# A hybrid decoder step: group norm moved into the next head pair's scan, and the last job cut into two token halves

## Chip, cores and metric

The kernel runs on one core of a Trainium2 chip. The metric is the device time of one execution in microseconds.

## The reference, cut to what matters

One inference step of one decoder layer, in float32, over 544 tokens (512 of a prompt, and 8 samples of 4 tokens). The width is 1024. Three branches run on the same normalised input: sparse attention (A), RWKV-7 time mixing (B) and cross attention into 256 memory tokens (C). Their outputs pass sigmoid gates and an output matrix, then a squared-ReLU MLP of width 4096 and a last RMS norm. The change touches branch B and the last norm:

```
def step(S, inp):                               # per head, 8 heads of 64
    sa = einsum('bhvk,bhk->bhv', S, -kk_t)
    S = S*w_t + sa (x) (kk_t*a_t) + v_t (x) k_t
    return S, einsum('bhvk,bhk->bhv', S, r_t)   # y
yn  = (y - mean(y)) * rsqrt(var(y) + GN_EPS) * ln_g + ln_b     # per head: "group norm"
out = (yn + sum(r*k*r_k)*v) * g                 # the sum term is the "bonus"
...
y_p = h_p + square(relu(rmsnorm(h_p, norm_mlp_g) @ w_mlp_up)) @ w_mlp_down
y_prompt = rmsnorm(y_p, norm_final_g)
```

## The kernel before

Activations lie with features on the 128 partitions and tokens along the free dimension (TOK = 544, HALF = 272, C = 64 tokens to a chunk, NCH = 8 chunks). Each engine has its own hand-written program, and they meet only through counting semaphores (`s["name"]`), so an engine that waits holds up all that is written behind the wait on that engine.

**Jobs.** All large matmuls are jobs of `JOBS`, each of 128 output features: `pb` (the RWKV projections), `gate` (24), `branch`, `out`, `up` and `down` (32, alternating in groups of 8). From `pb 6` on they are split: a weight slab lands by DMA, ScalarE makes its high part (`weights_hi`, L563), and GpSimd (`early_lo`, L577, up to the first `branch` job) or VectorE (`weights_lo`, L571, behind that) the low part, and every k tile takes three matmuls (L980 to L982; behind the scans L1539, L1540, L1543).

**Fills.** The `pb` and `gate` jobs of this region are not run in one piece. `fill_plan` cuts them into steps (one k tile of one half of the tokens, three matmuls of 272 columns for a split job) and deals them out over named places ("tags") in TensorE's program by a table of budgets; `fill(tag)` issues them. ScalarE moves a finished half out of PSUM in `evacs(tag)` (L1652 for the gates) at the matching place of its own program, and issues the `weights_hi` of a later job there; `split_tags` picks those places, and GpSimd calls `early_lo` for the same tags, between its other work, in order.

**The scan.** Branch B loops over four pairs of heads, j = 0 to 3. For each pair TensorE runs: *prep* (fills "prep" 0, 1, 3, 2, with the block sum of `rk` between them), the *pair stage* (matmuls of 64x64 that build and invert the chunk matrices, L1334 to L1415), the *chunks* (per chunk a chain: z matmuls L1424/L1428, ScalarE copies zs L1883, u matmuls L1437, ScalarE copies us L1888, state matmuls L1442, VectorE updates the state L2308, next chunk; with three fills each), the *decode stage* of the samples ("dec", L1466 to L1510, five fills) and *gn*, the group norm. `early(j + 1, ...)` makes the first inputs of the next pair in the chunks. `wide` (L1283) is a 128x128 float32 matmul over all tokens, and is used for block sums and small projections; its results lie in the PSUM pairs 0, 4 or 6.

**Group norm** (tag "gn"): TensorE `wide` of y (mean), VectorE subtracts (`yc`, L2346), ScalarE squares (L1914), TensorE `wide` (var), ScalarE square root (L1917), VectorE reciprocal (L2348), product (L2349), gain and shift (L2350), adds the bonus (L2351) and multiplies by g (L2353, `oB_out`). Behind that `oB_out` GpSimd begins `diff(r_, j + 1)` (L828 to L832) and behind its `diff` VectorE runs `mix` (L2176, L2179), the cumulative scan of the decays (L2252), the chunk offsets (L2256 to L2261, `lx`), ScalarE four exponentials (L1850 to L1853, `exps`), VectorE `rk` (L2264) and the factors (L2265 to L2269), TensorE the `rk` sum, VectorE the bonus (L2271), and only then the pair stage of the next pair.

**The end.** The last job (`down 31`) adds into its tile of `xT3` in one piece (L2417). ScalarE squares that tile, VectorE adds the squares of the tiles up (`add_square`, L1983), TensorE sums over partitions with a matrix of ones (L931), ScalarE takes the square root of all 128x544 (L1618), VectorE the reciprocal (L1965) and eight products (L1974), and SyncE stores each tile (L749).

## Time and profile before

| | us |
|---|---|
| median of three runs | 1272.91 |
| lowest, highest | 1270.98, 1279.83 |
| the profiled execution, its own time | 1272.74 |
| its span in the profile | 1271.1 |

The profile is of one execution; its own time is the span and 1.6 us around it. Stretches are given in microseconds from the start of the span. "PE" is TensorE's matmuls, "PEld" its weight loads, DVE is VectorE, ACT ScalarE, POOL GpSimd, SP SyncE. PEclk is the share of full clock (2.4 GHz) that TensorE was granted; 0.5 is 1.2 GHz. Idle time in brackets stands ahead of the instruction, with the one that released it.

### The profile page before, as it was taken

Reading aid. Unit: us, or ns where it says so; the run is one execution under the profiler, and the core shown is the slowest. Engines: PE = TensorE matmul, PEld = TensorE weight load, DVE = VectorE, ACT = ScalarE, POOL = GpSimd, SP = SyncE. Lnnn points to the kernel's source line nnn. Section 1 sums busy time; section 2 is a strip of 40 time slices with the busy share of each in tenths; the row PEclk is TensorE's granted clock in tenths of the full one; section 3 lists DMA queues with packets and bytes.
Section 4 is the critical chain, followed back from the end, with each engine's and each line's share of the span. In section 5 each row is a group of like instructions: output and inputs, shape, how many; then the busy total and the mean of one; then the engine's idle time right before and its main releaser. Section 6 shows DMA issues by size and latency. Waiting matters only on the chain.

```text
span 1271.1 us, 26790 instructions
## 1 busy us (share of the span) xinstructions
PE 1209.3 (95%) x11356; PEld 1077.9 (85%) x11359; DVE 661.1 (52%) x1190; ACT 385.7 (30%) x743; POOL 181.3 (14%) x218
## 2 busy tenths in 40 slices
PE   7999999898999899889989999999999999999994
PEld 5777665585887888887888899999999999999994
DVE  4898778440634534544362466656554254354334
ACT  2211333343532334333333342233232122122121
POOL 0414000111442242231142200000000000000000
PEclk9999999999999999989999999999999999999997
DMA  8234533233101111201211156522222222222101
GB/s 309 80 121 151 166 114 133 80 137 117 35 19 61 60 53 62 102 11 60 96 68 36 45 189 221 199 96 71 92 75 100 80 87 101 70 97 100 67 34 71
DMA packets 39178, 122.82 MB, mean 97 GB/s; under 512 B 5282, under 2 KB 16546, under 8 KB 30482
## 3 DMA queue, kind: packets, MB, share of 16 engines
q1 hardware_dynamic: 37106, 116.01, 26.2%
q0 software_dynamic: 1952, 5.09, 1.2%
q8 instruction: 90, 1.47, 0.5%
q14 instruction: 30, 0.25, 0.1%
HBM read 109.18 MB, written 11.90 MB: 95 GB/s over the span
## 4 chain that ended last, share of the span: by engine, by line
PE 86%; DVE 7%; issue 2%; ACT 2%; POOL 1%; DMA 1%; SPq 0%; DVEq 0%; ACTq 0%; POOLq 0%
PE ps L1540 13%; PE ps L1543 13%; PE ps L1539 13%; PE ps L989 7%; PE ps L980 5%; PE ps L947 5%; PE ps L981 3%; PE ps L982 3%; PE ps L1283 2%; PE ps L1107 2%; PE ps L1334 1%; PE ps L987 1%; PE ps L984 1%; PE ps L1371 1%; PE ps L1347 1%
## 5 line engine op out<-in xcount | busy, mean ns | idle before, releaser
L563 ACT ACTIVATE wh<-land 128x1024 fp32r<-128x1024 f32 (+1 forms) x125 | 122.1, 977 | 360.3 <-PE ps L1543 360.3
L571 DVE TENSOR_TENSOR wl<-land,wh 128x1024 fp32r<-128x1024 f32 (+1 forms) x94 | 103.3, 1099 | 149.7 <-ACT wh L563 149.0
L980 PE MATMUL ps<-xghi,wh 128*128 128x272 f32 x464 | 151.6, 327 | 9.8 <-ACT R L1652 8.5
L1539 PE MATMUL ps<-xhi,wh 128*128 128x272 f32 x512 | 138.3, 288 | 0.0
L1540 PE MATMUL ps<-hl,wh 128*128 128x272 f32 x512 | 138.2, 289 | 0.0
L1540 PE MATMUL ps<-xlo,wh 128*128 128x272 f32 x512 | 138.2, 289 | 0.0
L1539 PE MATMUL ps<-hh,wh 128*128 128x272 f32 x512 | 138.1, 288 | 0.0
L981 PE MATMUL ps<-xlo,wh 128*128 128x272 f32 x464 | 135.1, 291 | 0.0
L982 PE MATMUL ps<-xghi,wl 128*128 128x272 f32 x464 | 134.9, 291 | 0.0
L980 PEld LDWEIGHTS ps<-xghi,wh 128*128 128x128 f32 x464 | 88.9, 192 | 23.6 <-issue 14.3
L1543 PE MATMUL ps<-xhi,wl 128*128 128x272 f32 x512 | 106.1, 288 | 0.0
L1543 PE MATMUL ps<-hh,wl 128*128 128x272 f32 x512 | 106.1, 288 | 0.0
L577 POOL TENSOR_TENSOR wl<-land,wh 128x1024 fp32r<-128x1024 f32 (+1 forms) x31 | 73.1, 2359 | 226.6 <-ACT wh L563 226.6
L989 PE MATMUL ps<-xn,ring 128*128 128x272 f32 x384 | 98.2, 398 | 0.9 <-ACT aq L1769 0.9
L1540 PEld LDWEIGHTS ps<-xlo,wh 128*128 128x128 f32 x512 | 96.4, 188 | 0.0
L1540 PEld LDWEIGHTS ps<-hl,wh 128*128 128x128 f32 x512 | 96.4, 188 | 0.0
L1539 PEld LDWEIGHTS ps<-xhi,wh 128*128 128x128 f32 x512 | 96.3, 188 | 0.0
L1539 PEld LDWEIGHTS ps<-hh,wh 128*128 128x128 f32 x512 | 96.3, 188 | 0.0
L981 PEld LDWEIGHTS ps<-xlo,wh 128*128 128x128 f32 x464 | 89.1, 192 | 0.9
L982 PEld LDWEIGHTS ps<-xghi,wl 128*128 128x128 f32 x464 | 89.2, 192 | 0.0
L989 PEld LDWEIGHTS ps<-xn,ring 128*128 128x128 f32 x384 | 69.2, 190 | 17.5 <-issue 5.0
L1543 PEld LDWEIGHTS ps<-hh,wl 128*128 128x128 f32 x512 | 80.1, 188 | 0.0
(436 smaller groups left out, 2390.5 us busy)
## 6 DMA issues: line engine op xcount, KB each, us to landing
land<-in_slabs SPq DMA_DIRECT2D x51, 1024.0 KB, 4.8
ring<-in_slabs SPq DMA_DIRECT2D x14, 1024.0 KB, 5.4
gates<-R SPq DMA_DIRECT2D x24, 272.0 KB, 2.1
merge<-gates SPq DMA_DIRECT2D x24, 272.0 KB, 2.9
land<-in_slabs SPq DMA_DIRECT2D x12, 512.0 KB, 5.0
R<-in_kv SPq DMA_DIRECT2D x24, 128.0 KB, 2.0
pb<-in_kv SPq DMA_DIRECT2D x24, 128.0 KB, 2.0
xT<-in_xT SPq DMA_DIRECT2D x4, 544.0 KB, 6.9
```

Source lines behind the costliest of these rows:

```text
L563: act.activation(hi, src, ACT.Copy).then_inc(s["weights_hi"], 1)
L571: dve.tensor_tensor(lo, src, hi.bitcast(F32), ALU.subtract).then_inc(s["weights_lo"], 1)
L577: pool.tensor_tensor(lo, src, hi.bitcast(F32), ALU.subtract).then_inc(s["early_lo"], 1)
L947: mm = pe.matmul(ps[0:w, b + h, 0:HALF], W[:, k, c0_:c0_ + w], src[:, k, h * HALF:(h + 1) * HALF], start=(k == 0), stop=(k == KT - 1))
L980: pe.matmul(ps[:, b, 0:HALF], whi[:, k], hi, start=a, stop=False)
L981: pe.matmul(ps[:, b, 0:HALF], whi[:, k], lo, start=False, stop=False)
L982: mm = pe.matmul(ps[:, b, 0:HALF], wlo[:, k], hi, start=False, stop=z)
L989: mm = pe.matmul(ps[:, b, 0:HALF], W[:, k, c0_:c0_ + w], xn3[:, k, h * HALF:(h + 1) * HALF], start=a, stop=z)
L1107: pe.matmul(ps[:, 4 + u % 3, 0:P * (t + 1)], aq3[hp, ht, P * t:P * (t + 1)], ak[hp, 0:P * (t + 1)], start=True, stop=False)
L1539: pe.matmul(ps[:, b + h, 0:HALF], whi[:, k], hi[k][:, c], start=a, stop=False)
L1540: pe.matmul(ps[:, b + h, 0:HALF], whi[:, k], lo[k][:, c], start=False, stop=False)
L1543: mm = pe.matmul(ps[:, b + h, 0:HALF], wlo[:, k], hi[k][:, c], start=False, stop=z)
```

## The change

Nothing is computed differently, except that the two halves of the last norm go by another route to the same sum.

- **Fills.** The budgets of `fill_plan` change: prep of pairs 1 to 3 from 8+8+6+8 to 5+5+4+4 steps, each chunk from 2+2+2 to 2+3+3 (2 in the first place becomes 5 in chunk 4 of pairs 1 to 3; the last place of chunk 7 stays 5), each decode place from 4 to 5. The gn fills of pairs 0 to 2 go (6+6+10 each); those of pair 3 become 9+13+15, and nothing is left for the end.
- **Group norm of pairs 0 to 2** moves into the next pair. y and the bonus of pairs 0 to 2 get tiles of their own (`y_`, `bonus`, `var_`). TensorE: mean between prep 0 and prep 1, var ahead of chunk 0, g in chunk 5. ScalarE: the square behind the prep evacuations, the square root in chunk 0. VectorE: the subtraction ahead of the bonus, reciprocal in chunk 2, product in chunk 3, gain, shift and bonus in chunk 5, the product with g in chunk 6. The decode stage of TensorE waits for `oB_out`.
- **The next pair's preparation** moves ahead: GpSimd's `diff(r_, j + 1)` into the pair stage of pair j, VectorE's `mix` and scan into chunk 7, the chunk offsets behind the decode masks, ScalarE's exponentials into the decode stage, VectorE's factors behind the decode state. `fill("dec", j, 1)` moves ahead of the matmul of `ssq` (L1486).
- **Around it.** GpSimd calls `early_lo` of the prep tags inside the pair stage. ScalarE copies y ahead of the last evacuations of chunk 7. The high and low parts of the branch sources are made in another order, four in chunks 0 to 3 of pair 3, four in its decode stage (`SOURCE_ORDER`), and the first branch job waits for eight of them and not four.
- **The last job** is done as 24 matmuls for tokens 0 to 271, then 24 for the rest, with the first half's norm between these. Per half, the partition sums are formed with tokens on the output partitions (8 matmuls with one column), so root and reciprocal are of 68x4 elements, and 4 matmuls spread the result over 128x272. VectorE scales 16 half tiles; SyncE stores two half tiles at a time.

The diff, cut to its core (indentation shortened):

```diff
@@ -246,12 +246,12 @@
-    waits += [(("prep", j, n), b) for n, b in zip((0, 1, 3, 2), (8, 8, 6, 8) if j else (8, 22, 10, 8))]
+    waits += [(("prep", j, n), b) for n, b in zip((0, 1, 3, 2), (5, 5, 4, 4) if j else (8, 22, 10, 8))]
     if j < 3:
 waits += [(("need", "pb", 9 + j), 0)]
-    waits += [(("chunk", NCH * j + c, n), 5 if (c, n) == (NCH - 1, 2) else 2) for c in range(NCH) for n in range(3)]
-    waits += [(("dec", j, n), 4) for n in range(5)]
-    waits += [(("gn", j, n), b) for n, b in enumerate((6, 6, 10))]
+    waits += [(("chunk", NCH * j + c, n), (5 if j and c == 4 else 2, 3, 5 if c == NCH - 1 else 3)[n]) for c in range(NCH) for n in range(3)]
+    waits += [(("dec", j, n), 5) for n in range(5)]
+waits += [(("gn", 3, n), b) for n, b in enumerate((9, 13, 15))]
 waits += [(("need", "gate", 23), 0)]
 plan, done, at = {}, {}, 0
 for tag, budget in waits:
...
@@ -478,7 +479,11 @@
-    y_ = r_
+    y_ = [pb3[:, 4 + j, 0:TOK] for j in range(3)] + [r_]
+    bonus = [pb3[:, 8 + j, 0:TOK] for j in range(3)] + [L_]
+    kka = k__
     m4 = R[:, G:G + 2048].rearrange("p (n m t) -> p n m t", n=NCH, m=4)
-for k in range(KT):
-    sp.wait_ge(s["norm_out"], 17 + k)
-    sp.dma_start(o["yT"][:, k], cut(yo, 0, KT, TOK)[:, k]).then_inc(s["y_stored"], 16)
+for h in range(2):
+    c = slice(h * HALF, (h + 1) * HALF)
+    for k in range(0, KT, 2):
+        sp.wait_ge(s["norm_out"], 16 + KT * h + k + 2)
+        sp.dma_start(o["yT"][:, k:k + 2, c], cut(yo, 0, KT, TOK)[:, k:k + 2, c]).then_inc(s["y_stored"], 16)
...
@@ -844,20 +855,15 @@
+pool.wait_ge(s["t12"], 2)
+diff(r_, 0)
 for j in range(4):
-    if j:
-        pool.wait_ge(s["oB_out"], j)
-    else:
-        pool.wait_ge(s["t12"], 2)
-    diff(r_, j)
...
-    for n in splits(("prep", j, 0), ("prep", j, 1)):
-        early_lo(pool, n)
...
-    for n in splits(("prep", j, 3), ("prep", j, 2)):
+    for n in splits(("prep", j)):
         early_lo(pool, n)
...
         diff(k__, 5 + j)
         diff(v__, 9 + j)
+        pool.wait_ge(s["factors"], j + 1)
+        diff(r_, j + 1)
...
@@ -1306,17 +1314,22 @@
+        fill("prep", 0, 1)
+        fill("prep", 0, 3)
     else:
         fill("prep", j, 0)
-    fill("prep", j, 1)
-    fill("prep", j, 3)
+        pe.wait_ge(s["s_y_out"], j)
+        wide(0, k_("blk"), y_[j - 1]).then_inc(s["mean"], 1)
+        fill("prep", j, 1)
+        pe.wait_ge(s["sstate"], j)
     pe.wait_ge(s["rk"], j + 1)
     wide(6, k_("blk"), L_).then_inc(s["rk_sum"], 1)
+    if j:
+        fill("prep", j, 3)
+        pe.wait_ge(s["yc"], j)
     fill("prep", j, 2)
     if j < 3:
         fill("need", "pb", 9 + j)
-    if j:
-        pe.wait_ge(s["oB_out"], j)
     pe.wait_ge(s["factors"], j + 1)
...
@@ -1417,6 +1430,9 @@
+    if j:
+        pe.wait_ge(s["yc_sq"], j)
+        wide(0, k_("blk"), var_[j - 1]).then_inc(s["var"], 1)
...
@@ -1451,13 +1467,23 @@
         mm.then_inc(s["ychunk"], 1)
+        if j and c == 0:
+            fill("chunk", n, 2)
+            pe.wait_ge(s["y_rt"], j)
         if j < 3 and c in (0, 1, 3):
             early(j + 1, (0, 1, 0, 2)[c])
-        fill("chunk", n, 2)
+        if j and c == 5:
+            if j < 3:
+                pe.wait_ge(s["kk_rt"], j + 2)
+            wide(0, lora[:, 512 + P * (j - 1):512 + P * j], t13).then_inc(s["g"], 1)
+        if not (j and c == 0):
+            fill("chunk", n, 2)
...
-    if j < 3:
+    if j:
+        pe.wait_ge(s["oB_out"], j)
+    else:
         pe.wait_ge(s["kk_rt"], j + 2)
...
@@ -1481,11 +1507,11 @@
     mm.then_inc(s["s_z"], 1)
+    fill("dec", j, 1)
     pe.wait_ge(s["s_inv_out"], 4 * j + 2)
     for hh, hp, hs in HEAD:
         mm = pe.matmul(ps[hs, 7, 0:NS], ssq[hs], sx[hs], start=True, stop=True)
     mm.then_inc(s["s_inv"], 1)
-    fill("dec", j, 1)
     pe.wait_ge(s["s_z_out"], 2 * (j + 1))
     pe.wait_ge(s["s_inv_out"], 4 * (j + 1))
...
@@ -1511,15 +1537,15 @@
-    pe.wait_ge(s["s_y_out"], j + 1)
-    wide(0, k_("blk"), y_).then_inc(s["mean"], 1)
-    fill("gn", j, 0)
-    pe.wait_ge(s["yc_sq"], j + 1)
-    wide(4, k_("blk"), tA).then_inc(s["var"], 1)
-    fill("gn", j, 1)
-    pe.wait_ge(s["yc"], j + 1)
-    wide(6, lora[:, 512 + P * j:512 + P * (j + 1)], t13).then_inc(s["g"], 1)
-    fill("gn", j, 2)
...
+def split_by_half(n, src, h, ks):
...
+    hi, lo = src
+    for k in ks:
+        pe.matmul(ps[:, b + h, 0:HALF], whi[:, k], hi[k][:, c], start=(k == 0), stop=False)
+        pe.matmul(ps[:, b + h, 0:HALF], whi[:, k], lo[k][:, c], start=False, stop=False)
+        mm = pe.matmul(ps[:, b + h, 0:HALF], wlo[:, k], hi[k][:, c], start=False, stop=(k == KT - 1))
...
+def end_sum(h):
...
+        c = slice(h * HALF + QT * q, h * HALF + QT * (q + 1))
+        pe.matmul(ps[0:QT, 4 + h, q:q + 1], total[3][:, c], k_("ones")[:, 0:1], start=True, stop=False)
+        mm = pe.matmul(ps[0:QT, 4 + h, q:q + 1], nbuf[3][0][:, (KT - 1) % 2, c], k_("ones")[:, 0:1],
+                       start=False, stop=True)
+    mm.then_inc(s["norm_sum"], 1)
...
+    for q in range(4):
+        mm = pe.matmul(ps[:, 6 + h, QT * q:QT * (q + 1)], endr[0:QT, 4 * h + q:4 * h + q + 1].to_broadcast([QT, P]),
+                       ident[0:QT, 0:QT], start=True, stop=True)
+    mm.then_inc(s["norm_sum"], 1)
...
-        if idx == 31:
-            pe.wait_ge(s["norm_rt"], 3)
         split_job(n, H[r % 2])
-norm_sum(3)
+split_ready(NJOB - 1)
+split_by_half(NJOB - 1, H[1], 0, range(KT))
+split_by_half(NJOB - 1, H[1], 1, range(0, 3))
+pe.wait_ge(s["norm_rt"], 3)
+end_sum(0)
+split_by_half(NJOB - 1, H[1], 1, range(3, 6))
+end_spread(0)
+split_by_half(NJOB - 1, H[1], 1, range(6, KT))
+end_sum(1)
+end_spread(1)
...
@@ -1832,6 +1897,14 @@
+def exps(j):
+    act.wait_ge(s["lx"], j + 1)
+    act.activation(tA, L_, ACT.Exp).then_inc(s["exps"], 1)
...
@@ -1844,19 +1917,18 @@
-        evacs("prep", j, 0)
-    act.wait_ge(s["lx"], j + 1)
...
-    if j:
-        evacs("prep", j, 1)
-    evacs("prep", j, 3)
-    evacs("prep", j, 2)
+        for n in (0, 1, 3, 2):
+    if j:
+        act.wait_ge(s["yc"], j)
+        act.wait_ge(s["rk_sum"], j + 1)
+        act.activation(var_[j - 1], y_[j - 1], ACT.Square).then_inc(s["yc_sq"], 1)
...
+        if j and c == 0:
+            act.wait_ge(s["var"], j)
+            act.activation(h2(var_[j - 1]), pair(0), ACT.Sqrt, bias=gneps, scale=1.0 / 64).then_inc(s["y_rt"], 1)
-        if j == 3:
+        if j == 3 and c < 4:
...
+        if c == NCH - 1:
+            act.wait_ge(s["ychunk"], NCH * (j + 1))
+            act.activation(y_[j][:, 0:SEQ], ps[:, 5, :], ACT.Copy).then_inc(s["y_chunk"], 1)
-    act.wait_ge(s["ychunk"], NCH * (j + 1))
-    act.activation(y_[:, 0:SEQ], ps[:, 5, :], ACT.Copy).then_inc(s["y_chunk"], 1)
...
+    if j < 3:
+        exps(j + 1)
     evacs("dec", j, 2)
+    if j == 3:
+        act.wait_ge(s["oB_out"], 3)
+        for k in range(4, 8):
+            source_hi(act, k)
...
+end = evacuated(NJOB - 1, "v")
+for h in range(2):
...
+    act.wait_ge(s["evac_v"], end + h)
+    act.wait_ge(s["norm_ss"], KT * 4 - 2)
+    act.activation(nbuf[3][0][:, (KT - 1) % 2, c], xT3[:, KT - 1, c], ACT.Square).then_inc(s["norm_sq"], 1)
+    act.wait_ge(s["norm_sum"], 3 + 2 * h)
+    act.activation(endt[0:QT, 4 * h:4 * h + 4], ps[0:QT, 4 + h, 0:4], ACT.Sqrt, bias=epsc[0:QT],
+                   scale=1.0 / D).then_inc(s["norm_rt"], 1)
...
@@ -2242,33 +2332,63 @@
+def ahead(j, n):
+    if n == 0:
+        dve.tensor_tensor(kka, kk, a_, ALU.mult)
+        mix(r_, j, 4 + 3 * j)
+    elif n == 1:
+        step(dve.tensor_tensor_scan(L_, k_("reset"), lw, 0.0, ALU.mult, ALU.add))
     else:
-        dve.wait_ge(s["oB_out"], j)
...
+        step(dve.tensor_copy(c0, L_[:, C // 2 - 1:SEQ:C]))
...
+        dve.tensor_tensor(a_, L_, lw, ALU.subtract).then_inc(s["lx"], 1)
...
+def factors(j):
...
-    dve.tensor_copy(sdec, tA[:, SEQ + 3:TOK:4])
+    if j:
+        dve.wait_ge(s["s_y"], j)
+def group_norm(j, n):
+    y = y_[j]
+    if n == 0:
+        dve.wait_ge(s["mean"], j + 1)
+        dve.scalar_tensor_tensor(h2(y), pair(0), -1.0 / 64, h2(y), ALU.mult, ALU.add).then_inc(s["yc"], 1)
+    elif n == 1:
+        dve.wait_ge(s["y_rt"], j + 1)
+        step(dve.reciprocal(tB if j == 3 else var_[j], var_[j]))
+    elif n == 2:
+        step(dve.tensor_tensor(y, y, tB if j == 3 else var_[j], ALU.mult))
+    elif n == 3:
+        step(dve.tensor_scalar(y, y, v_("rwkv_ln_g", j), v_("rwkv_ln_b", j), ALU.mult, ALU.add))
+        step(dve.tensor_tensor(y, y, bonus[j], ALU.add))
+    else:
+        dve.wait_ge(s["g"], j + 1)
+        dve.tensor_tensor(h2(pb3[:, j, 0:TOK]), pair(6 if j == 3 else 0), h2(y), ALU.mult).then_inc(s["oB_out"], 1)
...
+    if j:
+        group_norm(j - 1, 0)
     dve.wait_ge(s["rk_sum"], j + 1)
-    dve.tensor_tensor(h2(L_), pair(6), h2(v__), ALU.mult).then_inc(s["bonus"], 1)
+    dve.tensor_tensor(h2(bonus[j]), pair(6), h2(v__), ALU.mult).then_inc(s["bonus"], 1)
...
+        if j and c in (2, 3, 5, 6):
+            group_norm(j - 1, (0, 0, 1, 2, 0, 3, 4)[c])
+        if j < 3 and c == NCH - 1:
+            ahead(j + 1, 0)
+            ahead(j + 1, 1)
+        if j == 3 and 1 <= c <= 4:
             source_lo(dve, c - 1)
-    if j == 3:
-        source_lo(dve, 7)
...
+    if j < 3:
+        ahead(j + 1, 2)
...
+    if j < 3:
+        factors(j + 1)
+        dve.wait_ge(s["sstate"], j + 1)
+        dve.tensor_copy(sdec, tA[:, SEQ + 3:TOK:4])
+group_norm(3, 0)
+for k in range(4, 8):
+    source_lo(dve, k)
+for n in range(1, 5):
+    group_norm(3, n)
...
+end_add(0)
+end_inverse(0)
+end_scale(0, range(0, 2))
+end_add(1)
+end_scale(0, range(2, 5))
+end_inverse(1)
+end_scale(0, range(5, KT))
+end_scale(1, range(KT))
```

`split_by_half(n, src, h, ks)` issues for each k the three matmuls of `split_step` for half h alone, and signals when the last k is through. `end_add(h)` adds PSUM into the last tile, `end_inverse(h)` is the reciprocal, `end_scale(h, ks)` the products of half h with the spread row in PSUM.

## Rows read from the trace of the kernel before

**Rows 1.** The page: TensorE's busy share, and its granted clock in 40 slices.
```profile
PE 1209.3 (95%) x11356; PEld 1077.9 (85%) x11359; DVE 661.1 (52%) x1190; ACT 385.7 (30%) x743; POOL 181.3 (14%) x218
...
PEclk9999999999999999989999999999999999999997
```

**Rows 2.** Windows: length, busy us of each engine, then PEclk, DMA share, GB/s.
```profile
398.00:412.30 14.30, 12.96 (x161) 10.27 (x160) 5.43 (x15) 4.12 (x11) 4.42 (x3) 1.00 0.22 77
...
412.30:443.50 31.20, 26.40 (x186) 25.30 (x188) 19.82 (x24) 10.32 (x18) 8.10 (x8) 0.95 0.17 60
...
466.00:502.00 36.00, 36.00 (x402) 29.92 (x398) 15.68 (x28) 14.67 (x32) 7.76 (x7) 1.00 0.27 91
...
515.90:550.30 34.40, 27.76 (x186) 26.23 (x186) 19.15 (x24) 12.88 (x19) 9.08 (x8) 0.90 0.29 102
...
572.00:610.50 38.50, 36.77 (x400) 30.29 (x396) 15.94 (x28) 14.09 (x32) 6.79 (x7) 0.96 0.17 58
...
627.00:657.70 30.70, 26.73 (x186) 25.23 (x186) 20.70 (x24) 11.54 (x18) 9.61 (x8) 0.94 0.29 105
...
728.30:741.50 13.20, 13.20 (x96) 12.52 (x95) 8.23 (x8) 5.93 (x8) 1.84 (x2) 1.00 0.25 82
...
868.40:1246.80 378.40, 376.34 (x2994) 376.15 (x2994) 166.54 (x196) 88.11 (x102) 0.00 (x0) 1.00 0.23 81
```

**Rows 3.** Waits of TensorE: who waited <- for whom: total us, times, longest.
```profile
PE ps L980 <- ACT R L1652: 8.5, 2, 4.8
...
PE ps L1283 <- DVE R L2264: 5.7, 1, 5.7
...
PE ps L1466 <- issue: 2.2, 3, 0.9
...
PE ps L1428 <- DVE small L2308: 1.5, 1, 1.5
...
PE ps L980 <- POOL wl L577: 1.2, 2, 1.0
```

**Rows 4.** Timeline of VectorE between pairs 0 and 1: start us, us, what.
```profile
418.77 3.55 DVE L2348 RECIPROCAL R<-R 128x544 f32<-128x544 f32 x1 [3.19 <-ACT R L1917]
...
428.08 2.39 DVE L2179 SCALAR_TENSOR_TENSOR R<-R,vec,pb 128x32 f32<-128x32 f32 x1
```

**Rows 5.** Timeline of GpSimd between pairs 1 and 2.
```profile
530.09 2.36 POOL L577 TENSOR_TENSOR wl<-land,wh 128x1024 fp32r<-128x1024 f32 x1 [8.85 <-ACT wh L563]
```

**Rows 6.** Timeline of ScalarE between pairs 1 and 2.
```profile
521.24 1.28 ACT L1917 ACT_TABLE_LOAD   x1
522.53 0.72 ACT L1917 ACTIVATE R<-ps,small 128x544 f32<-128x544 f32 x1
```

**Rows 7.** Timeline of TensorE and VectorE in the decode stage of pair 0.
```profile
403.26 0.14 PEld L1486 LDWEIGHTS ps<-R 32*32 32x32 f32 x4
...
403.56 0.39 DVE L2331 TENSOR_TENSOR R<-R,ps 32x32 f32<-32x32 f32 x2 [0.91 <-PE ps L1486]
```

**Rows 8.** Timeline of VectorE and GpSimd in the chunks of pair 2.
```profile
596.09 2.60 DVE L2205 TENSOR_SCALAR R<-R 128x544 f32<-128x544 f32 x1
598.72 3.55 DVE L2206 RECIPROCAL R<-R 128x544 f32<-128x544 f32 x1
...
596.02 2.37 POOL L577 TENSOR_TENSOR wl<-land,wh 128x1024 fp32r<-128x1024 f32 x1 [9.64 <-ACT wh L563]
```

**Rows 9.** Timeline behind the last job.
```profile
1252.94 0.72 DVE L2417 TENSOR_TENSOR xT<-ps,xT 128x544 f32<-128x544 f32 x1 [4.67 <-PE ps L1543]
...
1256.01 2.18 PE L931 MATMUL ps<-tail,cst 128*128 128x272 f32 x4 [3.11 <-DVE tail L1983]
...
1259.03 3.55 DVE L1965 RECIPROCAL tail<-tail 128x544 f32<-128x544 f32 x1 [3.07 <-ACT tail L1618]
...
1262.62 5.65 DVE L1974 SCALAR_TENSOR_TENSOR yo<-xT,vec,tail 128x544 f32<-128x544 f32 x8
```

**Rows 10.** Groups by shape, scan region: line, count, busy us, mean ns, idle before.
```profile
L2286 DVE TENSOR_TENSOR R<-R,ps 128x256 f32<-128x256 f32 x24 | 10.1, 421 | 31.5 <-PE ps L1371 22.5 <-PE ps L1378 9.1
```

More of the change, by code:

```diff
@@ L290, in split_tags @@
         tags += [("chunk", NCH * j + c, 2) for c in range(NCH)]
-        tags += [("dec", j, n) for n in (0, 2, 4)] + [("gn", j, n) for n in (1, 2)]
+        tags += [("dec", j, n) for n in (0, 2, 4)]
+    tags += [("gn", 3, n) for n in range(3)]
     order = {tag: n for n, tag in enumerate(FILLS)}
@@ L2270, in _ @@
+            for n in range(3, 7):
+                early(0, n)
+            for n in range(3):
+                ahead(0, n)
+            factors(0)
+            for j in range(4):
+                if j:
+                    group_norm(j - 1, 0)
                 dve.wait_ge(s["rk_sum"], j + 1)
-                dve.tensor_tensor(h2(L_), pair(6), h2(v__), ALU.mult).then_inc(s["bonus"], 1)
+                dve.tensor_tensor(h2(bonus[j]), pair(6), h2(v__), ALU.mult).then_inc(s["bonus"], 1)
+                if j == 0:
+                    dve.tensor_copy(sdec, tA[:, SEQ + 3:TOK:4])
```

116 lines of the change are left out of this document (69 added, 47 removed).

## The prediction

> **What bounds the kernel.** I began with the page [rows 1]: TensorE is busy for 95% of the span, and the granted clock shows one mark below 9 ahead of the end. The work is therefore TensorE's, and what an edit of order can return is its idle time and the time at half clock. The windows by stage [rows 2] show where that lies. Behind the scans (868 to 1247 us) 2994 matmuls take 376.34 us, 0.1257 us each, with nothing to gain. The fill steps of the scans are the same matmuls, so a step costs 0.377 us wherever it stands. The loss is between the pairs: 31.20 us with 26.40 busy, 34.40 with 27.76, 30.70 with 26.73. That is 4.80 + 6.64 + 3.97 = 15.4 us idle. The clock adds to it: PEclk 0.95, 0.90 and 0.94 leave 5, 10 and 6% of the three stretches as loss at half clock, 1.6 + 3.4 + 1.8 = 6.8 us. Behind the last pair (728 to 741 us) nothing is idle, although the same chain runs there: the fills cover it, and no next pair follows.
>
> The waits name the links [rows 3]. Fills waited for a ScalarE evacuation (8.5 us in two waits), the `rk` sum for VectorE's L2264 (5.7 us), and a fill for GpSimd's `early_lo` (1.2 us). These are in-order effects. In the boundary between pairs 0 and 1 VectorE begins the reciprocal at 418.77 and still mixes r at 428.08 [rows 4], and ScalarE, waiting for `lx`, leaves evacuations behind it. Between pairs 1 and 2 an `early_lo` begins only at 530.09, after 8.85 us of idle GpSimd [rows 5], and holds the `diff` behind it, on which all of the next pair hangs.
>
> The end is the other serial place [rows 9]: from the add at 1252.94 to the end of the span at 1271.1 there are 18.2 us with one engine at a time.
>
> **The sum for the scans.** Total work on TensorE is unchanged: the fill steps are only dealt out anew. Going by the code, a pair boundary now holds 5 (dec 4) + 18 steps and two `wide`. I walk the one behind pair 0 to 2 from the end of the L1510 matmuls as 0. VectorE's two state products end at 1.6 (0.7 each), `rk` and four factors (0.7 each) at 5.2. TensorE has the dec and the first prep steps and the mean (10 steps 3.8, a `wide` 0.9, change of tile shape some 0.3) at 5.0, prep 1 at 6.9, the `rk` sum at 7.8. The subtraction (VectorE, to 6.2) and the bonus (to 8.6) end before prep 3 and 2 do, at 10.8. So the pair stage starts without a wait, with 2 us in hand, and an `early_lo` of 2.4 us on the way would use this up and little more. All 22.2 us of boundary loss go. With them goes the wait of chunk 5 in pair 2: L1428 waited 1.5 us [rows 3], the window has 1.73 idle and PEclk 0.96, 3.2 us together; what comes back of this kind is counted below. Of the 2.2 us in three waits of L1466 at the start of the decode stage (ScalarE copies y last) 1.5 go, since the copy is moved ahead. Removed: 22.2 + 3.2 + 1.5 = 26.9 us.
>
> What the new order adds:
>
> - **Decode.** `fill("dec", j, 1)` now stands ahead of L1486, and nothing is left between L1486 and L1492, which needs VectorE's sum of it. In the trace L1486 starts at 403.26 and the two sums run from 403.56 for 0.39 us [rows 7], so TensorE goes on at about 404.0, some 0.65 us late, in each of four pairs: +2.6 us. The moved fill covers the chunk offsets (2.1 us on VectorE), which stand ahead of the `ssq` copies: TensorE needs 3.5 us from the masks to L1486. If offsets were longer than that, L1486 would wait by the difference.
> - **ScalarE in chunk 0.** Copy `us`, table load 1.28, root 0.72 [rows 6], and for pairs 1 and 2 again a load of 1.28 ahead of the tanh (0.7), and a `weights_hi` (1.05) ahead of the next `zs`. TensorE has the third fill ahead of `y_rt` (1.13 us and its small matmuls, 2.3 us behind `us`), so it waits about 0.3 us for the root, and about 0.9 for `zs` of chunk 1: 2 x 1.2 + 0.3 = +2.7 us. Queued behind the root are `zs` and every evacuation; all are in this sum. Bounds: 0, and 2 x 3 + 1 = 7.
> - **VectorE in the chunks.** A reciprocal takes 3.55 [rows 8] and stands ahead of the state update of the next chunk. A chunk was 36/8 = 4.5 us [rows 2] and has two more steps now, 5.2, and 6.3 in chunk 4. State, decay and the reciprocal are 4.7, so chunk 2 has 0.5 us to spare, chunk 4 has 1.6. The trace shows what spoils that: a TENSOR_SCALAR of 0.44 us took 2.60 beside `early_lo` (2.37) [rows 8], and a mix of 32 columns 2.39 [rows 4]. One uncovered case in three pairs with one reciprocal each is what the trace has; I take two among the six reciprocals, 1.6 us each and one spell of half clock among them less what chunk 4 covers: +3 us. Bounds: 0, and 6 x 1.6 + 3 x 1.7 = 15.
> - **var ahead of chunk 0** stands between small matmuls where its old place was between fills: two changes of tile shape, three times, +0.6 us; bounds 0 and 1. g in chunk 5 stands beside a fill: nothing.
> - **Elsewhere.** The mix and scan (3.0 us) in chunk 7 are covered by 5 fills and the first decode matmuls (3.3 us), and the masks behind them by 5 dec fills (1.9 against 1.4); with an `early_lo` across them up to 1.4 us appear per pair, and I count none because L1466 already lost its wait. The exponentials (2.1 us) delay evacuations in the decode stage, but a half's bank is needed one half (3 us) later. GpSimd's `diff(r_)` is made a stage early, ahead of the state load and `early_lo`, 1.5 us with a stage of slack. Source parts of pair 3 lie in ScalarE and VectorE idle time, and the stricter wait for 8 is met before the 16.7 us of the last gn fills are over: nothing.
>
> Together +8.9, net **-18.0 us**.
>
> On the collisions between VectorE and GpSimd the Trainium skill, "SBUF — State Buffer", section "SBUF: two separate sides", calls their shared port pair an exclusive lock that also catches a VectorE operation with two SBUF inputs. The 2.60 and 2.39 us agree. By that rule the moved products and scans are targets too, and the sum would stand nearer the upper bound of that term, some 3 us worse.
>
> For the table load the same skill, "ScalarE: Activation LUTs", section "What ACT_TABLE_LOAD costs", adds a drain of about 1.38 us to each load. Here the root starts at 522.53, right behind the load of 521.24 plus 1.28 [rows 6], so no drain is seen. By the page chunk 0 would cost five loads more of that size, +7 us, and the total would be near 1255.
>
> **The sum for the end.** The last job's 48 matmuls take 6.03 us and ended at 1252.9, so they began at 1246.9. Half 0 is through at 1249.9. VectorE adds 272 columns: 256 columns take 0.42 [rows 10], and back to back 544 columns go at 5.65/8 = 0.706 [rows 9], so I take 0.36 per half tile in a row. Add to 1250.4, square to 1250.8; TensorE comes to the sums at 1251.05. The small matmuls are not in the trace: per pass the bounds are 0.25/4 = 0.06 us [rows 7] and 2.18/4 = 0.55 [rows 9]; I take 0.06 to 0.07, since they have one to 68 columns, as the first. 16 passes end at 1252.1, root and reciprocal of 4 columns at 1252.6, behind nine job matmuls; the spread (8 passes) ends at 1253.9, the job at 1254.75. VectorE: two products, the second add to 1255.2, three products to 1256.3. Second chain: square 1255.6, sums 1256.7, root and reciprocal 1257.2, spread 1257.8; VectorE meanwhile three products to 1258.3, then eight to 1261.2. Before, the last product ended at 1268.3 and the span 2.8 us later. With the same 2.8 the span ends at 1264.0. The stores now have runs of half the length; I allow 0.5 for that, 1264.5: **-6.6 us**. Bounds: -8.5 with every wait covered, -3 with passes of 0.2 us and slower stores.
>
> **Result.** 1272.74 - 18.0 - 6.6 = 1248.1 us. The profiled execution lies 0.2 below the median, so the forecast is 1248.
>
> **The rivals.**
>
> - *The covers hold throughout:* none of the 8.9 us returns. 1272.7 - 26.9 - 6.6 = 1239. For it: most chunks of the trace have no wait. Against: L1486 to L1492 has nothing between them. Chance 0.12.
> - *ScalarE and VectorE take half back:* the upper bounds of the two chunk terms nearly hold (7 and 12), with clock loss, 1254 to 1260. For it: ScalarE then carries two table loads in one chunk. A pause of 1.4 us behind each table load would give 1255 as well; it has 0.01 of this, since [rows 6] show 0.01 us between load and root. Chance 0.14.
> - *The stall only moves:* one boundary wait returns at another place, such as a fill that waits for `early_lo`, because the prep tags' calls now stand behind `dlow` and `m4`. Against: by the new plan their jobs are first needed in the chunks (gate 2 in chunk 0 of pair 1), and the rest of the pair stage lies between. If this margin were gone, each pair would lose some 5 us, as at the boundary of pair 0, and 1.7 of clock: 1248 + 20 = 1268, or no change. Chance 0.06.
> - *Slower:* VectorE becomes the head of the chunk chain. Every chunk now has a long operation behind the state update, and GpSimd makes about eight `early_lo` a pair. Each that hits uncovered costs 1.6 us, and with its share of half clock 1.9. From 13 uncovered hits on, 24.6 us are used up; at 25 of 32 the time is 1248 + 22 x 1.9 = 1290. Against: VectorE was busy for 15.7 of 36 us in the chunks of pair 1 [rows 2], and the moved work adds 10 us to a stage of 42. Chance 0.03.
>
> The forecast's own case (1241 to 1254) has 0.65. The range for eight in ten reaches from the better rival into the half-back one: 1239 to 1257. A difference of 1% (12.7 us) is about what a measurement of this kernel tells from none. Faster by more needs less than 1260.2: 0.91; within 1% 0.06; slower 0.03.
>
> **What the changed profile would show.** Boundaries: TensorE busy as long as the stretch, PEclk 1.00, no wait of a fill for L1652 and none of the `rk` sum. Decode: a new wait before L1492 of about 0.6 us, four times. Chunk 0: a table load and a root on ScalarE, and a short wait of TensorE behind. Chunks 2 and 4 of each pair: reciprocals with the state update on time, or a wait near 1.6 us where `early_lo` crosses. End: some 10 us from the last job matmul to the end where 18.2 were, the job itself some 1.9 us longer for what stands between, and the half tiles 0.36 us apart. The forecast would be wrong if half clock stays in these windows, if chunks take over 5.6 us, or if the last stores land later than 4 us behind the last product.

## The result, and the profile after

| | before | after |
|---|---|---|
| median, lowest, highest of six runs (us) | 1274.55, 1270.98, 1279.83 | 1259.53, 1255.84, 1264.34 |
| the profiled execution, its own time | 1272.74 | 1255.84 |
| its span | 1271.1 | 1254.2 |

The ratio of the times is 0.989 (95% interval 0.986 to 0.991). The forecast was 1248 with a range of 1239 to 1257: the direction was right, the gain was 15.0 us where 24.6 were forecast, and the median lies 2.5 us above the range. Beside its own profile the gain is 16.9 us. The six runs after differ in the granted clock: the mean over the span is 0.993 in the fastest and 0.988 in the slowest, which is 8.8 and 15.1 us lost to it (1 less the clock, times the span), 6.3 of the 8.5 us between the two.

To see where the time went I cut both spans at four events: the first pair-stage matmul of pair 0, the first matmul of the first `branch` job, VectorE's add of the job `down 30`, and the end.

| stretch | before | after | change | forecast |
|---|---|---|---|---|
| to the first pair stage | 337.7 | 336.9 | -0.8 | 0 |
| the scans, to the first branch matmul | 404.5 | 392.6 | -11.9 | -18.0 |
| on to the add of `down 30` | 504.7 | 506.1 | +1.4 | 0 |
| on to the end | 24.2 | 18.6 | -5.6 | -6.6 |

The page of the changed kernel, TensorE's line and the clock, beside [rows 1]:

```profile
PE 1207.6 (96%) x11403; PEld 1077.0 (86%) x11403; DVE 651.4 (52%) x1199; ACT 387.2 (31%) x747; POOL 180.6 (14%) x218
...
PEclk9999999999999999999999999999999999999998
```

Windows by stage (length, busy us of PE, PEld, DVE, ACT, POOL, then clock, DMA share, GB/s). These answer to [rows 2]; the second, fourth and sixth row are the boundaries behind pairs 0 to 2, each from the masks of the decode stage to the next pair stage:

```profile
398.00:403.90 5.90, 5.90 (x71) 5.22 (x66) 2.81 (x6) 2.38 (x7) 0.00 (x0) 1.00 0.39 161
403.90:429.90 26.00, 24.00 (x235) 21.03 (x235) 14.74 (x30) 9.03 (x20) 5.77 (x4) 1.00 0.19 64
466.00:502.00 36.00, 35.61 (x383) 31.03 (x383) 19.41 (x30) 14.46 (x29) 7.10 (x3) 1.00 0.25 83
502.00:527.90 25.90, 23.87 (x233) 20.93 (x232) 14.68 (x30) 7.82 (x18) 5.79 (x4) 1.00 0.25 86
572.00:601.00 29.00, 28.62 (x309) 24.94 (x309) 17.04 (x25) 11.73 (x25) 7.11 (x3) 1.00 0.16 57
601.00:627.50 26.50, 24.47 (x247) 21.45 (x243) 15.18 (x30) 8.32 (x18) 5.79 (x4) 1.00 0.34 123
```

The clock is 1.00 in all of them, and a boundary holds 2.0 us of idle time where it held 4.8, 6.6 and 4.0. The chunks in the third and fifth row lose 0.4 us; both rows begin behind chunk 1, whose wait comes below. Now the waits of TensorE, beside [rows 3] (waited for: us, times, longest):

```profile
PE ps L1501 <- DVE R L2448: 5.7, 4, 1.4
PE ps L1453 <- ACT R L1955: 5.2, 11, 1.8
...
PE ps L1518 <- DVE R L2456: 2.3, 4, 0.6
PE ps L939 <- DVE tail L2073: 2.1, 1, 2.1
```

No row of [rows 3] is left: no fill waits for a gate evacuation, no `rk` sum for VectorE. In their place stand the inverse products of the decode stage (L1501, L1475 before) that wait for VectorE's masks in each pair, the u matmuls of a chunk (L1453) that wait for `zs` (L1437 before), and L1518 (L1492 before). The first is the one that I had counted at nothing. VectorE and GpSimd around it in pair 0:

```profile
402.75 1.28 DVE L2341 TENSOR_TENSOR_SCAN R<-cst,R 128x544 f32<-128x544 f32 x1
404.07 0.28 DVE L2444 TENSOR_TENSOR R<-ps,cst 32x128 f32<-32x128 f32 x1
404.28 0.17 DVE L2446 TENSOR_TENSOR R<-ps,cst 32x32 f32<-32x32 f32 x1
404.48 2.11 DVE L2448 TENSOR_TENSOR R<-R,cst 32x32 f32<-32x32 f32 x1
...
407.05 0.18 DVE L2448 TENSOR_TENSOR R<-R,cst 32x32 f32<-32x32 f32 x1
...
410.97 0.39 DVE L2456 TENSOR_TENSOR R<-R,ps 32x32 f32<-32x32 f32 x2 [1.21 <-PE ps L1513]
```

```profile
404.18 2.37 POOL L586 TENSOR_TENSOR wl<-land,wh 128x1024 fp32r<-128x1024 f32 x1 [7.78 <-ACT wh L572]
```

L2448 is the sum behind the two mask products (`sm4` plus the identity, 32x32). It takes 2.11 us for the first head and 0.18 for the second. Both its inputs are in SBUF; the two products before it read PSUM and run at their usual 0.28 and 0.17, although GpSimd's low part began at 404.18. The slow one ends at 406.59, some 0.04 us behind the low part (404.18 + 2.37). TensorE then begins L1501 1.42 us late:

```profile
407.29 0.25 PE L1501 MATMUL ps<-R 32*32 32x32 f32 x4 [1.42 <-DVE R L2448]
...
411.51 0.30 PE L1518 MATMUL ps<-R 32*32 32x64 f32 x4 [0.59 <-DVE R L2456]
```

All four pairs have it (1.42 to 1.44), pair 3 too, ahead of whose masks no mix or scan stands. The low part is the one of the last chunk tag in `split_tags`, released by the `weights_hi` of that place; so it meets the masks each time.

The kernel before already had the same meeting, in pairs 0 and 3. Its waits and, in pair 0, its sum (L2325) and low part:

```profile
PE ps L1475 <- DVE R L2325: 0.9, 2, 0.4
```

```profile
400.28 0.98 DVE L2325 TENSOR_TENSOR R<-R,cst 32x32 f32<-32x32 f32 x1
```

```profile
398.85 2.37 POOL L577 TENSOR_TENSOR wl<-land,wh 128x1024 fp32r<-128x1024 f32 x1 [8.69 <-ACT wh L563]
```

There the low part began 1.0 us ahead of the first mask product, and only its last 0.94 us fell on the sum. In the changed kernel it begins 0.1 us behind that product and nearly all of it falls on the sum; ScalarE now copies y ahead of the last `weights_hi` of chunk 7.

ScalarE in chunk 0 and 1 of pair 2, the same within 0.01 in pair 1:

```profile
554.34 1.28 ACT L1964 ACT_TABLE_LOAD   x1
555.63 0.71 ACT L1964 ACTIVATE R<-ps,small 128x544 f32<-128x544 f32 x1
557.66 1.28 ACT L1863 ACT_TABLE_LOAD   x1 [1.31 <-PE ps L1291]
558.96 0.71 ACT L1863 ACTIVATE R<-ps,small 128x544 f32<-128x544 f32 x1
559.57 1.05 ACT L572 ACTIVATE wh<-land 128x1024 fp32r<-128x1024 f32 x1
560.51 0.21 ACT L1955 ACTIVATE R<-ps 128x64 f32<-128x64 f32 x1
```

Root with its load, tanh with its load, then `weights_hi` (L572), and only then `zs` (L1955). TensorE waits 1.75 us for it, and in pair 2 a spell of 3.4 us at half clock began 0.4 us behind the wait, at 561.2.

The end, VectorE, TensorE (last spread) and the stores, beside [rows 9]:

```profile
1242.99 0.91 DVE L2563 SCALAR_TENSOR_TENSOR yo<-xT,vec,ps 128x272 f32<-128x272 f32 x2 [1.61 <-PE ps L1601]
1243.81 0.43 DVE L2552 TENSOR_TENSOR xT<-ps,xT 128x272 f32<-128x272 f32 x1
...
1246.30 0.17 DVE L2556 RECIPROCAL tail<-tail 68x4 f32<-68x4 f32 x1 [0.83 <-ACT tail L2042]
...
1247.88 3.36 DVE L2563 SCALAR_TENSOR_TENSOR yo<-xT,vec,ps 128x272 f32<-128x272 f32 x8 [0.19 <-PE ps L1601]
```

```profile
1244.86 0.25 PE L1592 MATMUL ps<-cst,tail 128*68 128x1 f32 x2 [1.09 <-ACT tail L2040]
...
1246.53 1.31 PE L1601 MATMUL ps<-cst,tail 68*128 68x68 f32 x8 [0.56 <-DVE tail L2556]
```

```profile
1243.92 7.71 SPq L760 DMA_DIRECT2D out_yT<-yo  x8
```

The reciprocal of 68x4 elements takes 0.17 us where 128x544 took 3.55. The last product ends at 1251.24 and the span 2.96 us later.

### The profile page after: what moved, and what is told of

The parts are those of the page before. It is cut to its first block, busy times and chain, and to the rows that moved or that the text cites. A ratio compares the mean times of both kernels' runs of the same rounds, so it can differ in the third digit from the quotient of the medians.

```text
span 1254.2 us, 26903 instructions
## 1 busy us (share of the span) xinstructions
PE 1207.6 (96%) x11403; PEld 1077.0 (86%) x11403; DVE 651.4 (52%) x1199; ACT 387.2 (31%) x747; POOL 180.6 (14%) x218
## 4 chain that ended last, share of the span: by engine, by line
PE 88%; DVE 6%; issue 2%; ACT 2%; DMA 1%; SPq 0%; DVEq 0%; ACTq 0%
PE ps L1566 13%; PE ps L1565 13%; PE ps L1569 13%; PE ps L997 6%; PE ps L988 5%; PE ps L955 5%; PE ps L990 4%; PE ps L989 4%; PE ps L1291 2%; PE ps L1115 2%; PE ps L1347 1%; PE ps L995 1%; PE ps L992 1%; PE ps L1384 1%; PE ps L1360 1%
## 5 line engine op out<-in xcount | busy, mean ns | idle before, releaser
L572 ACT ACTIVATE wh<-land 128x1024 fp32r<-128x1024 f32 (+1 forms) x125 | 121.9, 976 | 361.2 <-PE ps L1569 361.2
L988 PE MATMUL ps<-xghi,wh 128*128 128x272 f32 x464 | 148.4, 320 | 0.0
L1566 PE MATMUL ps<-hl,wh 128*128 128x272 f32 x496 | 133.8, 289 | 0.0
L1565 PE MATMUL ps<-hh,wh 128*128 128x272 f32 x496 | 133.8, 288 | 0.0
L1569 PE MATMUL ps<-hh,wl 128*128 128x272 f32 x496 | 102.8, 288 | 0.0
L1566 PEld LDWEIGHTS ps<-hl,wh 128*128 128x128 f32 x496 | 93.4, 188 | 0.0
L1565 PEld LDWEIGHTS ps<-hh,wh 128*128 128x128 f32 x496 | 93.3, 188 | 0.0
L1569 PEld LDWEIGHTS ps<-xhi,wl 128*128 128x128 f32 x512 | 80.6, 189 | 0.0
```

The costliest lines, as they stand in the source:

```text
L572: act.activation(hi, src, ACT.Copy).then_inc(s["weights_hi"], 1)
L988: pe.matmul(ps[:, b, 0:HALF], whi[:, k], hi, start=a, stop=False)
L1565: pe.matmul(ps[:, b + h, 0:HALF], whi[:, k], hi[k][:, c], start=a, stop=False)
L1566: pe.matmul(ps[:, b + h, 0:HALF], whi[:, k], lo[k][:, c], start=False, stop=False)
L1569: mm = pe.matmul(ps[:, b + h, 0:HALF], wlo[:, k], hi[k][:, c], start=False, stop=z)
```

## The experiments

Single times are told beside the after profile (1255.84), and the stretches and waits come from each run's own trace. "Scans" and "end" are the stretches of the table above.

**1. The low part moved off the masks.** GpSimd's `early_lo` of the last chunk tag waits until the masks are done.

```diff
...
+                pool.wait_ge(s["s_m4"], 6 * (j + 1))
+                for n in splits(("chunk", NCH * (j + 1) - 1)):
+                    early_lo(pool, n)
```

> The changed kernel, but GpSimd's last low part of each pair's chunks waits until the decode masks are done. Theory (the low part locks VectorE out for its 2.4 us just as the mask sum of the decode stage, L2448 there, is due, so that sum takes 2.1 to 2.4 us where 0.18 is its length): the sum takes 0.2 us, the four waits of 1.4 us on TensorE ahead of the first inverse matmul go, scan region 5.8 us shorter. Rival (the masks are late because mix and scan were put ahead of them in chunk 7): the waits stay at 1 us or more in pairs 0 to 2 and only pair 3 changes. Second rival (the later low part makes a fill of the prep stage wait): the four waits go and new ones of 1 us or more come before a fill.

Measured: 1255.19 us, scans 390.1 (-2.5). The wait behind the masks is gone from all four pairs, which shows its cause. But the low part then ran into the next operation of VectorE with two SBUF inputs, the offset product:

```profile
406.08 0.18 DVE L2451 TENSOR_TENSOR R<-R,cst 32x32 f32<-32x32 f32 x1
406.30 0.17 DVE L2347 COPY small<-R 128x8 f32<-128x8 f32 x1
406.50 2.75 DVE L2349 TENSOR_TENSOR R<-R,small 128x512 f32<-128x512 f32 x1
```

It took 2.75 us for 0.69, the copies for the `ssq` matmul stand behind it, and TensorE waited 0.68, 0.62 and 0.62 us there in pairs 0 to 2. One more spell of half clock (1.7 us) came with it: -5.7 + 1.9 + 1.7 = -2.1 against -2.5 measured. The collision had moved, not gone.

**2. The decode fill cut in two**, half of it ahead of the `ssq` matmul and half behind.

```diff
-                fill("dec", j, 1)
+                fill("dec", j, 1, part=slice(0, 3))
                 pe.wait_ge(s["s_inv_out"], 4 * j + 2)
...
                 mm.then_inc(s["s_inv"], 1)
+                fill("dec", j, 1, part=slice(3, None))
```

> The changed kernel with the five fill steps of the second decode place dealt 3 ahead of the ssq matmul and 2 behind it. Theory (the wait behind that matmul, 0.59 us in each pair, is there because nothing lies between): the four waits go, 2.4 us in all, and the ssq copies are still in time (they ended 0.9 us before the matmul, two steps are 0.75). Rival (chunk offsets ahead of the ssq copies are too long for three steps): a wait of up to 0.3 us per pair appears ahead of the ssq matmul and half of the gain is given back.

Measured: 1258.76 us, scans 392.6. The wait of 0.59 us is gone four times, and from L1501 to the matmul of L1518 it is 3.76 us where it was 4.22: the cut gives 0.46 each, 0.13 less than the wait. What is new beside it are two more changes between large and small matmuls; that they are the 0.13 is my reading. The 1.8 us do not show in the stretch, because this run had one half-clock spell more in chunk 1 of pair 1 (465.7).

**3. The high part behind `zs`.** In chunk 0 of pairs 1 to 3 ScalarE's last evacuations and `weights_hi` go behind the `zs` copy of chunk 1.

```diff
+                    if j and c == 1:
+                        evacs("chunk", n - 1, 2)
...
-                    evacs("chunk", n, 2)
+                    if not (j and c == 0):
+                        evacs("chunk", n, 2)
```

> The changed kernel, with ScalarE's high part of a weight slab (1.05 us) that follows the tanh of chunk 0 moved behind the zs copy of chunk 1, in pairs 1 and 2. Theory (in chunk 0 ScalarE has two table loads, root, tanh and the high part in a row, 6.7 us, ahead of zs): the waits of TensorE for zs of chunk 1, 1.75 us in two pairs, fall to 0.7, 2.1 us in all, and the spell at half clock that followed the second one may go too (1.7 us). Rival (TensorE waits for the tanh and its table load for another reason, such as the product in PSUM): the waits stay at 1.7.

Measured: 1255.64 us, scans 389.1 (-3.5). The two waits of 1.75 us are 0.8 us each, and the spell at 561 is absent: 1.9 + 1.7 = 3.6 us. For the remaining 0.8 the trace shows, in pair 2, ScalarE idle for 1.31 us until TensorE's L1291 is done, then the load of 1.28 us and the tanh of 0.71 ahead of `zs`. So this wait is put down to the tanh and its load; TensorE did not wait for the root. No run tests it.

**4. All three.**

> The three edits of the other runs together on the changed kernel. Theory (three causes that do not overlap, 5.8 + 2.4 + 2.1 us and one spell at half clock): 10 to 12 us under the changed kernel, 1248 or so against its 1259.5 and 1274.5 of the kernel before, a ratio of 0.979 to 0.982 to before. Rival (the time missing from the forecast lies in the clock and in other places, and a wait that goes is replaced by the next link): under 5 us, a ratio of 0.985 or more.

Measured: median 1250.71 us (1247.12 to 1252.14, six runs), 0.982 of before (0.979 to 0.985); scans 387.0. The waits in the scan region:

```profile
PE ps L1516 <- DVE R L2460: 4.2, 3, 1.4
PE ps L1456 <- ACT R L1959: 3.3, 11, 0.8
```

The first is worse than in experiment 1: two steps (0.75 us) fewer stand ahead of L1516 to cover the slow offset product, and 0.68 us became 1.45 in pair 0. A spell of half clock followed that wait at 410.7. I had expected three causes that do not overlap and 1248 us; the first edit and the cut of the fill do overlap. VectorE and GpSimd:

```profile
405.92 2.75 DVE L2353 TENSOR_TENSOR R<-R,small 128x512 f32<-128x512 f32 x1
```

```profile
405.76 2.36 POOL L586 TENSOR_TENSOR wl<-land,wh 128x1024 fp32r<-128x1024 f32 x1 [8.98 <-DVE R L2455]
```

**5 and 6. One half alone.** The kernel before with the new last job and norm, and the changed kernel with the old ones.

```diff
@@ end_only: before, plus
+split_by_half(NJOB - 1, H[1], 0, range(KT))
...
@@ old_end: after, with
+norm_sum(3)
```

> The kernel before with the new last job and final norm alone; scans, order and fills as before. Theory (the end is worth what the profile of the changed kernel shows, 18.6 us from the start of the last job to the end of the span where 24.2 were): 5.6 us under before, a ratio of 0.9956. Rival (the forecast's 6.6 us hold and the changed kernel's end lost 1 us to the clock): 6.6 us or more, and a stretch of 17.6. Second rival (shorter runs of bytes make the stores the bound): under 4 us.

> The changed kernel with the end of the kernel before; scans as changed. Theory: the scan region takes 392.6 us as in the changed kernel, and 24.2 us pass from the start of the last job to the end of the span, so a span 5.6 us over the changed kernel's, 1259.8 if the spells at half clock are the same. Rival (both parts touch, through the clock or weights): the stretch is off by over 1 us.

Measured: the new end alone has a median of 1268.58 us (eight runs), 0.995 of before (0.993 to 0.997), -5.5 us. Its waits in the scan region are those of [rows 3] in each number, with other line numbers:

```profile
PE ps L984 <- ACT R L1695: 8.5, 2, 4.8
PE ps L1287 <- DVE R L2315: 5.7, 1, 5.7
PE ps L1470 <- issue: 2.2, 3, 0.9
PE ps L1432 <- DVE small L2359: 1.5, 1, 1.5
```

The old end on the changed kernel gave 1263.21 us, with a last stretch of 24.17, the same as before, and scans of 392.5, the same as after. So neither part changes the waits of the other: -5.6 of the end and -11.9 of the scans in the profiles of before and after. The end-only kernel's own last stretch is 19.2 and not 18.6. In the ten profiles with the new end it lies between 18.4 and 19.2, with 8.0 us of TensorE's idle time in each; the rest of the difference is where half clock begins. So the end is worth 4.9 to 5.8 us. The end-only kernel also had more half clock than before in the same places of the scans (23.9 us of spells there, before 17.1).

**7. The chunks without their added steps.** The budgets of the chunks go back to 2+2+2, and the steps go to the decode stage (the budgets alone are shown).

```diff
-(5 if j and c == 4 else 2, 3, 5 if c == NCH - 1 else 3)[n]
+(2, 2, 5 if c == NCH - 1 else 2)[n]
-(("dec", j, n), 5)
+(("dec", j, n), 8 if n == 1 else 9 if j else 8)
```

> The changed kernel with two steps in every place of a chunk (five in the last) as before, and the steps that this frees, 18 a pair, in the decode places. Theory (a chunk of 5.2 us covers the reciprocal that stands ahead of the state update, one of 4.5 us does not: state, decay and reciprocal are 4.7): new waits ahead of the matmul that needs the state (old L1428) in chunks 3 and 5 of pairs 1 to 3, 0.2 to 0.5 us each and about 2 us where a low part crosses, and the wait for zs in chunk 1 grows by 0.4; scan region 2 to 6 us longer. Rival (the new chunk budgets are idle ornament; the same steps in the decode stage do as well): region 392.6 within 1 us.

Measured: 1257.79 us, scans 394.0 with 10.2 us of half clock in one spell. The chunks lost little, in places other than those forecast:

```profile
PE ps L1453 <- ACT R L1955: 4.3, 4, 1.8
PE ps L988 <- POOL wl L586: 3.5, 4, 1.3
```

Six steps in a chunk cover a reciprocal of 3.55 us as well as eight do: no chunk waits for VectorE. The one new wait behind it, 0.60 us in chunk 3 of pair 2, is for `zs`, and the trace has ScalarE's `weights_hi` (575.64, 1.05 us) ahead of that copy. My account of the cover, by which VectorE had 0.5 us to spare in an eight-step chunk, falls: it was too strict. The wait behind the masks is gone here too, with eight or nine steps over it. Four new waits came for GpSimd's low parts, as jobs are needed at other times. Taking the half clock out of both (5.1 and 1.7 us), the scans are 388.9 and 390.9: taken as a whole, the steps added to the chunks gained nothing. But this run has got rid of the 5.7 us behind the masks and the changed kernel has not. Experiment 9, rid of them too, though with the offsets moved as well, comes to 384.4, 4.5 less than here, and most of that is the 3.5 us of waits for low parts. So the steps were not needed for the reciprocals, and their place still matters for the low parts.

**8. The offsets moved as well.** The three mends, and the chunk offsets go behind VectorE's sums for L1518, so that the low part meets none of the decode stage's chain.

```diff
-                if j < 3:
-                    ahead(j + 1, 2)
                 dve.wait_ge(s["s_inv"], 2 * j + 1)
...
                     dve.tensor_tensor(sxt[hs], sx[hs], ps[hs, 7, 0:NS], ALU.add).then_inc(s["s_inv_out"], 1)
+                if j < 3:
+                    ahead(j + 1, 2)
```

> The three mends, and VectorE's chunk offsets moved from ahead of the ssq copies to behind the sums that L1518 of the changed kernel waits for. With three mends the low part starts 0.1 us behind the masks and the offset product beside it took 2.75 us for 0.69, so the ssq copies came 1.4 us late in pairs 0 to 2. Theory (it is the lock again, one place further on; copies and sums with an operand in PSUM do not meet it): the three waits of 1.4 us go, 4.2 us and a spell at half clock (1.7), about 1245 and a ratio of 0.978. Rival (offsets so late delay the exponentials and the factors): the waits turn up at the pair stage or ahead of the decode state matmuls, and the time stays at 1250.

Measured: median 1246.12 us (1243.12 to 1247.20, five runs), 0.979 of before (0.977 to 0.981); scans 381.2 in the profiled run, 11.4 less than after. VectorE in pair 0, to be held against the row of 404.48 above:

```profile
403.31 0.18 DVE L2455 TENSOR_TENSOR R<-R,cst 32x32 f32<-32x32 f32 x1
...
407.56 0.39 DVE L2461 TENSOR_TENSOR R<-R,ps 32x32 f32<-32x32 f32 x2 [2.23 <-PE ps L1516]
407.98 0.17 DVE L2351 COPY small<-R 128x8 f32<-128x8 f32 x1
408.19 0.69 DVE L2353 TENSOR_TENSOR R<-R,small 128x512 f32<-128x512 f32 x1
```

The window of the boundary behind pair 0, masks to pair stage:

```profile
400.20:426.80 26.60, 26.60 (x261) 23.40 (x262) 15.24 (x34) 10.83 (x23) 5.75 (x4) 1.00 0.18 63
```

TensorE has no idle time in it. By the waits removed, 5.7 + 4 x 0.46 + 1.9 + 1.7 = 11.1 us. The median is 4.6 us below that of the three mends, whose waits of 4.2 us are gone.

**9. Low part and offsets alone**, fill and high part as in the changed kernel.

> The changed kernel with only two edits: the low part waits for the decode masks, and the chunk offsets stand behind the sums of the inverse. Theory (the 1.4 us ahead of the first inverse matmul are the lock and nothing else, and what came back when only the low part was moved was the lock on the offset product): none of the four waits of 1.4 us and none of the three of 0.65, region 5.8 us under the changed kernel's 392.6 at equal spells of half clock; the 0.59 us behind ssq and the 1.75 us of chunk 1 stay. Rival (late offsets delay exponentials and factors): a wait ahead of the rk sum or of a fill for an evacuation.

Measured: 1253.73 us; the wait behind the masks and that of the offset product are both gone, L1518's 0.59 and the 1.75 us of chunk 0 stayed. Scans 389.5, with a half-clock spell of 10.2 us at 462.4, 1.0 us behind that wait in pair 1. Without the half clock of both (5.1 and 1.7 us) the step is 384.4 against 390.9, -6.5, where the waits alone are 5.7; the other 0.8 are not explained.

**10. The whole decode fill behind the `ssq` matmul**, with the other mends.

```diff
-                fill("dec", j, 1)
                 pe.wait_ge(s["s_inv_out"], 4 * j + 2)
...
                 mm.then_inc(s["s_inv"], 1)
+                fill("dec", j, 1)
```

> The kernel of four mends, but with all five steps of the second decode place behind the ssq matmul, as in the kernel before, and none ahead. From the inverse matmul L1504 to the one of u TensorE took 4.22 us in the changed kernel and 3.76 with steps on both sides, where it changes tile shape once more. Theory (the ssq copies end 0.4 us behind the first inverse matmuls' results while the zaa matmuls run for 1.1, so no cover is needed ahead): 3.5 us a pair, 1 us in all under the four mends, within its noise in time. Rival (the copies are late without a fill): a wait ahead of the ssq matmul of 0.3 us or more, and no gain.

Measured: median 1245.33 us (1243.12 to 1245.83, five runs), 0.977 of before (0.975 to 0.979); scans 380.8. From the inverse products to the matmul of L1518 it is 3.57 us (4.22 in the changed kernel, 3.76 with the fill on both sides), without a wait. The intervals of 8 and 10 overlap, so the last 0.8 us between the medians are not shown. Either is 13 to 14 us below the changed kernel.

## Why the prediction was wrong

**The step that failed** is in the part "Elsewhere": "with an `early_lo` across them up to 1.4 us appear per pair, and I count none because L1466 already lost its wait". The size of the event was right, 1.42 to 1.44 us; the reason for counting none was not. The wait of L1466 was for ScalarE's copy of y and stands ahead of the masks' matmuls; removing it brings the masks no cover. And I treated the crossing as an accident, while GpSimd's last low part of the chunk tags is released at a fixed place of ScalarE's program and meets the masks every time. It costs 5.7 us, nearly the whole of the 6.1 that the scans fell short. Experiments 1, 8 and 9 show the cause. The trace of before had the warning, the wait of L1475 for L2325, 0.9 us in two pairs, which I passed over.

The Trainium skill, "SBUF — State Buffer", section "SBUF: two separate sides", says that the pair of ports is held exclusively and that VectorE operations with two SBUF inputs are caught. The runs agree: 0.18 became 2.11 to 2.35 us, 0.69 became 2.75, and operations with a PSUM operand beside them kept their time. I had cited the rule and priced it on the chunks, where it cost nothing. Two SBUF inputs are not the whole of it: the TENSOR_SCALAR of [rows 8], which I counted as agreement, has one tensor input and took 2.60 us for 0.44.

**The boundaries: right.** The 22.2 us of idle time and half clock left as forecast, with chunk 5's 3.2 and L1466's 1.5. TensorE had no idle time ahead of the pair stage in any of the three.

**What came back, by terms:**

| term | forecast | measured |
|---|---|---|
| masks beside a low part | 0 | 5.7 |
| L1486 to L1492 | 2.6 | 2.3 |
| ScalarE in chunk 0 | 2.7 | 3.5, and 1.7 of half clock |
| VectorE's reciprocals in the chunks | 3 | 0 |
| nine shorter waits of L1453 for `zs` | not counted | 1.3 more |
| place of var | 0.6 | not separated |

The nine waits are 5.2 - 3.5 = 1.7 us in the row above; the trace of before has two for the same link:

```profile
PE ps L1437 <- ACT R L1883: 0.4, 2, 0.2
```

Together, with 0.6 taken for the last row, 15.1 us come back, and 26.9 - 15.1 = 11.8 where 11.9 were measured. That this closes within 0.1 is partly luck. The 26.9 leaves out 0.7 us more of L1466 and the 0.9 of L1475, and counts 1.0 us twice, half clock that fell into idle time. Over the whole stretch TensorE's idle time went from 23.3 to 16.3 us, and what half clock took while it worked from 7.5 to 1.7. That is 12.8 less, where the stretch is 11.9 shorter, so about 1 us came back as longer work, in which the 0.6 for var is not separated. One term holds: the 0.65 us of the decode stage was 0.58 to 0.59, and experiments 2 and 10 removed it. The chunk 0 term had the right links, `weights_hi` among them, and the wrong sizes: a single wait for `zs` of 1.75 us in each of two pairs, where I had 0.9 and with it 0.3 for the root, which never was waited for. Experiment 3 halves it. The root begins at 555.63, where the load of 554.34 and 1.28 us ends; so the drain that the Trainium skill, "ScalarE: Activation LUTs", section "What ACT_TABLE_LOAD costs", adds to a load is not seen here either. VectorE's collisions in the chunks did not occur, and experiment 7 shows that my margins there were too small. (The half-back rival takes 12 us as the upper bound of that term, the term itself 15; neither was reached.)

**The end: right in kind, 1.0 us short.** -5.6 for -6.6, shown by experiments 5 and 6 (0.8 to 1.7 short over the ten profiles). The last spread of eight passes took 1.31 us, partly at half clock, where I had 0.6, and a half tile 3.36/8 = 0.42 where I had 0.36 (+0.5 over eight). The passes of the sums took 0.06 as taken. The stores ended 2.96 us behind the last product for 3.3 forecast.

**The rest.** +1.4 us lie between the scans and the last job. After a wait of 2.07 us for VectorE (2.06 before) a spell of half clock follows at 858.2, which costs 1.7. Of the twelve profiles eight have it, the new end on the old scans among them, and four don't, those of before and of experiments 1, 4 and 7. So it goes with the run and is not shown to be the change's; that before's one profile had none flatters it. I took the profiled execution to be 0.2 us below the median; after the change it was the fastest of six and 3.7 below (before, 1.8 below the median of six). The profiled run lies within the range and the median does not. With a difference of 0.2 the median would have been 1256.0, and without the wait behind the masks 1253.8: either would have brought it inside, so that it missed the range by 2.5 us took the failed step and the spread between runs together.

## What to carry to other kernels

When an engine's small operation on the critical chain has two SBUF inputs, look for what GpSimd is released to do at that place of the program: here a low part of 2.4 us stopped it for all that was left of the low part, every time and not now and then. A meeting that costs 0.4 us in two of four places in the profile before can cost 1.4 in all four when an edit shifts the two against each other. Moving the offender is enough only if the next such operation behind it is free too, so move it and read the timeline again. And count a wait as cover for another only if it stands on the same side of the chain.
